# Prompt attention of a latent-attention layer: three entries of the table that places side pieces between attention units

## The reference

```python
q = einsum('ntq,qhe->nthe', c_q, w_uq)           # queries of the head
s = (q_lat . c_kv + q_pe . k_pe) * SOFTMAX_SCALE # causal scores, masked
p = softmax(s)
o = p @ c_kv                                     # then o @ w_uv, and all heads @ w_o
```

## Time and profile before

| | kernel before |
|---|---|
| median of three runs | 2475.5 us |
| the profiled execution | 2474.55 us |
| its span | 2472.8 us |
| PE busy | 2397.4 us (97%) |
| DVE busy | 1087.5 us (44%) |
| ACT busy | 555.4 us (22%) |

### The profile page before, as it was taken

The page is one execution under the profiler, slowest core; times in us unless marked ns, Lnnn a source line. Parts: engine busy times, 40 slices in busy tenths (PEclk is TensorE's granted clock), DMA queues, the critical chain, the costliest instruction groups (busy, mean ns, idle before and its releaser), DMA issues.

```text
span 2472.8 us, 36121 instructions
## 1 busy us (share of the span) xinstructions
PE 2397.4 (97%) x13411; PEld 2136.1 (86%) x13411; DVE 1087.5 (44%) x2021; ACT 555.4 (22%) x990; POOL 724.0 (29%) x472
## 2 busy tenths in 40 slices
PE   8999999999999989899999998989999999999996
PEld 8899999999999978578888886679999999999995
DVE  4443443343344362335545565442433443443446
ACT  3411111111111153232222234633111111111112
POOL 3522232232222270021111113643322222223235
PEclk9999999999999989999999999999999999999998
DMA  5111101111111110100000013412011111101111
GB/s 198 43 48 51 51 25 51 51 34 43 51 41 35 51 41 19 39 13 14 26 18 18 10 52 104 120 51 69 27 49 51 46 30 51 51 25 51 51 34 73
DMA packets 132609, 117.92 MB, mean 48 GB/s; under 512 B 9056, under 2 KB 119608, under 8 KB 132512
## 3 DMA queue, kind: packets, MB, share of 16 engines
q1 hardware_dynamic: 132528, 116.84, 15.2%
HBM read 110.95 MB, written 6.42 MB: 47 GB/s over the span
## 4 chain that ended last, share of the span: by engine, by line
PE 90%; DVE 3%; ACT 2%; issue 1%; DMA 0%; SPq 0%; DVEq 0%; POOL 0%; ACTq 0%
PE ps L735 23%; PE ps L736 23%; PE ps L737 23%; PE ps L1099 3%; PE ps L1003 2%; PE ps L1086 2%; PE ps L973 1%; PE ps L1017 1%; PE ps L1149 1%; PE ps L1008 1%; PE ps L1049 1%; PE ps L1044 1%; PE ps L1052 1%; PE ps L1053 1%; PE ps L1050 1%
## 5 line engine op out<-in xcount | busy, mean ns | idle before, releaser
L735 PE MATMUL ps<-XH,WGH 128*128 128x368 f32 (+1 forms) x2112 | 695.2, 329 | 4.9 <-DVE XL L1616 3.2
L736 PE MATMUL ps<-XL,WGH 128*128 128x368 f32 (+1 forms) x2112 | 695.8, 329 | 0.0
L737 PE MATMUL ps<-XH,WGL 128*128 128x368 f32 (+1 forms) x2112 | 693.8, 328 | 0.0
L1703 DVE TENSOR_TENSOR XR<-XR,ps 128x512 f32<-128x512 f32 x756 | 511.2, 686 | 8.6 <-PE ps L737 4.2
L1686 DVE TENSOR_TENSOR HF<-SG,ps 128x368 f32<-128x368 f32 x132 | 70.7, 535 | 907.4 <-PE ps L737 894.7
L735 PEld LDWEIGHTS ps<-XH,WGH 128*128 128x128 f32 x2112 | 397.4, 188 | 9.2 <-DVE XL L1616 3.8
L736 PEld LDWEIGHTS ps<-XL,WGH 128*128 128x128 f32 x2112 | 396.9, 188 | 1.8
L737 PEld LDWEIGHTS ps<-XH,WGL 128*128 128x128 f32 x2112 | 397.2, 188 | 0.0
L737 PE MATMUL ps<-WDH,HL 128*128 128x512 f32 (+1 forms) x792 | 313.6, 396 | 0.0
L736 PE MATMUL ps<-WDL,HH 128*128 128x512 f32 (+1 forms) x792 | 311.9, 394 | 0.0
L735 PE MATMUL ps<-WDH,HH 128*128 128x512 f32 (+1 forms) x792 | 310.8, 392 | 0.0
(11 more groups left out here) (234 smaller groups left out, 3002.4 us busy)
## 6 DMA issues: line engine op xcount, KB each, us to landing
RAWG<-ffn_w_gate SPq DMA_DIRECT2D x44, 512.0 KB, 5.9
RAWG<-ffn_w_up SPq DMA_DIRECT2D x44, 512.0 KB, 6.9
RAWD<-ffn_w_down SPq DMA_DIRECT2D x44, 512.0 KB, 3.4
CR<-cache_mla_l SPq DMA_DIRECT2D x64, 160.0 KB, 2.5
XR<-x_prompt SPq DMA_DIRECT2D x8, 512.0 KB, 11.0
WOR<-mla_w_o SPq DMA_DIRECT2D x8, 512.0 KB, 3.4
o_y_prompt<-XR SPq DMA_DIRECT2D x8, 512.0 KB, 2.6
WOA<-mla_w_o SPq DMA_DIRECT2D x7, 512.0 KB, 4.7
```

The source lines that it names most:

```text
L735: pe.matmul(out, w[0], x[0], start=start, stop=False)
L736: pe.matmul(out, w[0], x[1], start=False, stop=False)
L737: return pe.matmul(out, w[1], x[0], start=False, stop=stop)
L1703: dve.tensor_tensor(XR[0:r, t, ds], XR[0:r, t, ds], ps[0:r, 4 + 2 * w + half, :], ALU.add).then_inc(s_row[2 * l + 1], 1)
```

## The change

Three entries of the table change, for the units 7, 0 and 6.

```diff
-NEXT_PLAN = (("", "a7 b6", "p7"), ("p6 p7 a6 b7", "", ""), ("p7", "a7 b6", ""), ("", "a7 b6", "p7 p6"),
+NEXT_PLAN = (("", "a6 b7", "p6 p7"), ("p6 a7", "", "b7"), ("", "a7 b6", "p7"), ("", "a7 b6", "p7 p6"),
              ("p7", "a6 b7", "p6"), ("p7", "a6 b7", "p6 p7"), ("a6 b7", "", ""), ("", "a7 b6", ""))
```

## The result

| | before | changed |
|---|---|---|
| median | 2475.87 us (6 runs) | 2485.4 us (6 runs, 2484.85 to 2487.04) |
| ratio | | 1.0037, 95% interval 1.0027 to 1.0047 |
| span of the profiled execution | 2472.8 us | 2485.2 us |
| one head (1 to 6) | 56.46 us | 57.86 us |

What follows compares the result with a forecast made beforehand. PE's stream, busy 97% of the span, was taken to bound the kernel. Terms of -1.16, +0.79 and -0.15 us gave -0.52 a head, -3.1 in six, +0.1 in the last: median 2472.5 us, range 2469.8 to 2476.0.

Steps and rivals of the forecast that it cites:

- the side to which I gave a chance of 0.03: Whole kernel: a loss of over 5.0 us, more than the two slower cases price; chance 0.03.
- PE's order up to T0 and the swap of banks, nothing: Unit 7, banks 6 and 7 swapped: no cost up to T0, the moment the first output piece starts.
- The new wait at unit 3's scores: Bank 6 holds the third query piece, so PE waits for `QTL` ahead of these scores: 0.44 us in place of 0.68.
- the 0.3 to 0.5 that I gave as a sign: Sign in the changed profile: matmul idle of 0.3 to 0.5 us at L1044 in each of six heads.
- The values 3.26 us behind T0: Sign at unit 0: its values start about 3.26 us behind the first output piece's start, in place of 4.42.
- The output piece behind the values, 0.79: Second output piece, put behind the values: the same three matmuls add 0.79 us to a head.
- The key piece, 1.18 out and in, and the wait for `ORW` hidden: Key piece behind unit 6's values: 1.18 us leaves and comes back, PE's wait for `ORW` is filled, -0.15 us.
- Bank 7 covered by 0.04 us: Unit 3's output piece: the key piece's evacuation frees bank 7 after 2.53 us, PE needs it after 2.57.
- The gain of a head, 0.52: Sum of the terms in each of the heads 1 to 6: -1.16 + 0.79 - 0.15 = -0.52 us.
- The `OTL` that releases unit 3's values would end some 0.2 us before PE comes there: DVE's chain behind `KTL` at unit 3, additional sum some 0.2 us: ends some 0.2 us ahead of PE's need.
- The rival "slower": `KTH` late, so `KTL` holds up DVE ahead of unit 3's sums and `OTL`: 2478.8 us; chance 0.05.
- The flush between DVE's operations: Rival: a pause behind each DVE operation adds 0.81 us in the chain to the values: 2477.3 us; chance 0.03.

Runs made afterwards that it cites:

- e6: The kernel before with only the key piece moved behind unit 6's values and GpSimd's subtraction one unit later; 2475.89 us, ratio 0.9998.
- e1: The changed kernel with the sum of the two partial sums written with one tensor input and a per-partition scalar; 2473.26 us, ratio 0.998.
- e2: The changed kernel with GpSimd's subtraction for the rotary queries one unit later, the two-input sum untouched; 2471.84 us, ratio 0.9979.
- e7: The changed kernel with the two-input sum moved on VectorE ahead of the key piece's `KTL`, GpSimd untouched; 2473.02 us, ratio 0.9989.
- e3: The kernel before with the key piece alone moved behind unit 6's values, query and output pieces as before; 2489.12 us, ratio 1.0048.
- e4: The kernel before with GpSimd's subtraction one unit earlier, so that it runs at unit 3's sum in its old place; 2475.91 us, ratio 1.0001.
- e5: The changed kernel with GpSimd's subtraction one unit later and a one-input cast of the rotary queries in its place; 2476.35 us, ratio 0.9999.

## Why the prediction was wrong

The measured 2485.4 us lies outside the range, on the side to which I gave a chance of 0.03. Step by step:

- *PE's order up to T0 and the swap of banks, nothing:* right. The first output piece starts right behind the query pieces, without a wait.
- *The new wait at unit 3's scores:* right. They start 1.66 us behind T0 (1195.28 - 1193.62), as worked out. The idle in the row is 0.19 us, under the 0.3 to 0.5 that I gave as a sign: a row counts it from the end of the matmul before, the 0.44 of the sum from where the next one could have started.
- *The values 3.26 us behind T0:* right to the last digit (1196.88 - 1193.62).
- *The output piece behind the values, 0.79:* 0.78 (1197.32 to 1198.10). But it starts 0.44 us behind the values (1196.88 to 1197.32), where the key piece before started 0.52 behind them (1193.41 to 1193.93): 0.08 that the sum did not have.
- *The key piece, 1.18 out and in, and the wait for `ORW` hidden:* 1.18 (1204.18 to 1205.36); unit 3's transposes and the start of its scores are 0.58 apart (1205.36 to 1205.94) in place of 0.71. Of the forecast 0.15 only 0.07 is left in the head's length, in e6.
- *Bank 7 covered by 0.04 us:* right. `KTL` ends at 1206.65, and the output piece starts at 1206.77 with no wait, 2.59 us behind the key piece where 2.57 was worked out.
- *The gain of a head, 0.52:* the three kernels without the overlap (e1, e2, e7) have 56.46 - 55.92 = 0.54, and their medians lie 3.4, 4.8 and 3.1 us below the kernel before beside them, where the forecast was 3.0. That the sum fits so closely is in part luck: the two entries of the query and output pieces gave 0.47 for the forecast 0.37, the key piece 0.07 for 0.15.
- *"The `OTL` that releases unit 3's values would end some 0.2 us before PE comes there":* wrong, and this is the step that failed. I put the sum in this chain at some 0.2 us. That is what it takes while GpSimd is idle (0.15 at 1200.29), and without the overlap `OTL` indeed ends ahead of PE, by 0.55 us in e2 (1205.71 and 1206.26). Beside GpSimd's subtraction it took 2.41 us, `OTL` ended at 1209.91 where PE could have gone on at 1208.21, and a head paid 1.94 us: six heads 11.6, against a gain of 3.2, +8.4 us by the heads (+9.5 by the medians; the other 1.1 is not located).

The rival "slower" had the place, DVE's chain behind `KTL` ahead of unit 3's values, but another mechanism (`KTH` late) and a price of a third; none of the rivals held GpSimd. I followed PE, DVE and ACT to the new place, and did not ask what GpSimd runs there. Both rows were in the trace of before, 1.93 us apart (1200.29 and 1202.22), and rows of that trace would have shown that they meet. GpSimd's subtraction starts 1.05 us behind the start of unit 3's transposes (1202.22 - 1201.17 before, 1206.41 - 1205.36 after). With the key piece of 1.18 us in front that is 2.23 us behind the key piece's start, and `KTL`, which the sum stands behind, ends only 2.47 us behind it (1207.67 - 1205.20).

The flush between DVE's operations, the rival from the rule, did not happen: the values came where the rows put them, not 0.81 us later. The section of the Trainium skill that the prediction cites for it ("VectorE: DVE Perf Modes", "The DRAIN you can't avoid") adds a sentence that the prediction left out: "A next op that is not held starts earlier". That is in keeping with the rows of the changed kernel too, where the addition starts 0.46 us behind the start of a `QTL` of 0.54 us (1195.14 and 1194.68).

The rule that does describe the loss stands in the Trainium skill, "SBUF — State Buffer", section "SBUF: two separate sides": VectorE and GpSimd share a pair of SBUF ports, and whichever of a two-SBUF-input VectorE operation and a GpSimd operation that reads SBUF starts first keeps it for the whole instruction. The runs agree: the sum ended within 0.03 us of the GpSimd operation in all six heads of the changed kernel, e3, e4 and e5, beside a subtraction and beside a cast, and with one tensor input it did not wait (0.21 us, e1). In all of them GpSimd started first; the case in which VectorE does, and a GpSimd operation that only writes, no run shows.

## What to carry to other kernels

Before an instruction is moved, list what each other engine runs at its new place, not only what it waits for: here a VectorE operation on one column with two SBUF inputs took 2.4 us because it fell into a GpSimd operation, and it stood on the way to the engine that sets the time. Such a sum is safer with one tensor input and a per-partition scalar (+0.06 us, 0.21 against 0.15), or ahead of the piece that makes it late. A gain that is worked out from distances in the timeline can be right in its sum and still be lost at an instruction that the change doesn't name. In the list of waits that instruction does not appear either: PE's wait there names `OTL`, four DVE instructions behind the sum, and the sum shows only as a long row.

## What the runs showed of the hardware

I had not expected that so short an operation could be held until a GpSimd instruction ends: 2.41 us for one element in each partition (usual 0.15), 0.94 us beside a cast, 1.33 us where it came later in the subtraction. Inside the same subtraction VectorE's operations with one input in PSUM keep their times: an addition to `XR` 0.64 us (e4), `OTL` 0.29 us (the row at 1202.49 in the kernel before; 0.29 outside it too, at 1209.62 in the changed one).
